# The last K tile of an fp32 operand's low part at another place within 256 bytes

## The reference

```python
u = x @ w_in                                  # 2048 -> 6144 columns
mix = concatenate([a_out, b_out]) @ w_out     # 2048 -> 2048
x = layer_norm(ALPHA * x + mix)
h = square(relu(x @ mlp_w1)) @ mlp_w2         # 2048 -> 8192 -> 2048
x = layer_norm(ALPHA * x + h)
```

## Time and profile before

| | |
|---|---|
| median of 3 runs | 2264.65 us |
| the profiled execution, its own time | 2263.86 us |
| its span, first to last instruction | 2262.1 us |
| PE busy | 2230.1 us, 99% |
| DVE busy | 1334.3 us, 59% |
| ACT busy | 1043.3 us, 46% |
| mean share of the DMA engines, first queue | 55.4% |
| granted TensorE clock, mean | 0.996 |

### The profile page before, as it was taken

The page is one execution under the profiler, slowest core; times in us unless marked ns, Lnnn a source line. Parts: engine busy times, 40 slices in busy tenths (PEclk is TensorE's granted clock), DMA queues, the critical chain, the costliest instruction groups (busy, mean ns, idle before and its releaser), DMA issues.

```text
span 2262.1 us, 36589 instructions
## 1 busy us (share of the span) xinstructions
PE 2230.1 (99%) x14395; PEld 2022.1 (89%) x14395; DVE 1334.3 (59%) x1472; ACT 1043.3 (46%) x1133; POOL 36.5 (2%) x68
## 2 busy tenths in 40 slices
PE   8999999999999999999999999999999999999998
PEld 8998888798898899899889999888989988988986
DVE  4999977854544545444565455568555454545455
ACT  4555565454444344354434444444544444544542
POOL 2000000000000001000000000000000000000000
PEclk9999999999999999999999999999999999999999
DMA  6555535565656566555536655564656566555553
GB/s 234 177 161 153 183 131 166 185 218 195 203 188 211 199 197 197 201 179 195 187 125 201 186 169 169 166 215 153 215 191 196 196 216 203 185 187 197 178 195 112
DMA packets 213081, 419.17 MB, mean 185 GB/s; under 512 B 12793, under 2 KB 13361, under 8 KB 211904
## 3 DMA queue, kind: packets, MB, share of 16 engines
q1 hardware_dynamic: 210832, 406.37, 55.4%
q0 software_dynamic: 1808, 10.04, 1.3%
q10 hardware_dynamic: 288, 0.52, 0.1%
HBM read 414.79 MB, written 2.10 MB: 184 GB/s over the span
## 4 chain that ended last, share of the span: by engine, by line
PE 92%; DVE 5%; issue 1%; DMA 1%; ACT 1%; SPq 0%; DVEq 0%; ACTq 0%
PE gemm L1343 15%; PE gemm L1345 15%; PE gemm L1344 15%; PE gemm L1367 14%; PE gemm L1370 14%; PE gemm L1369 14%; DVE lnp L1087 2%; DVE w_lo L806 1%; PE pair L1506 1%; DMA raw<-in_ev_w_in 1%; PE pair L1467 0%; DMA raw<-in_mlp_w 0%; PE pair L1565 0%; PE pair L1637 0%; PE pair L1610 0%
## 5 line engine op out<-in xcount | busy, mean ns | idle before, releaser
L1216 DVE TENSOR_TENSOR w_lo<-raw,w_hi 128x1024 fp32r<-128x1024 f32 x488 | 594.5, 1225 | 560.4 <-ACT w_hi L719 545.3
L1367 PE MATMUL gemm<-x_hi,w_hi 128*128 128x256 f32 x2944 | 824.9, 280 | 4.6 <-DVE w_lo L806 2.4
L719 ACT ACTIVATE w_hi<-raw 128x1024 fp32r<-128x1024 f32 x492 | 518.3, 1060 | 672.2 <-PE gemm L1345 375.4
L1370 PE MATMUL gemm<-x_hi,w_lo 128*128 128x256 f32 x2944 | 822.5, 279 | 0.1
L1369 PE MATMUL gemm<-x_lo,w_hi 128*128 128x256 f32 x2944 | 822.4, 279 | 0.0
L1367 PEld LDWEIGHTS gemm<-x_hi,w_hi 128*128 128x128 f32 x2944 | 554.2, 188 | 7.6 <-issue 2.9
L1370 PEld LDWEIGHTS gemm<-x_hi,w_lo 128*128 128x128 f32 x2944 | 560.8, 190 | 0.3 <-issue 0.3
L1369 PEld LDWEIGHTS gemm<-x_lo,w_hi 128*128 128x128 f32 x2944 | 554.7, 188 | 0.5
L1343 PE MATMUL gemm<-w_hi,c_hi 128*128 128x512 f32 x1280 | 501.0, 391 | 1.3 <-DVE w_lo L806 1.0
L1344 PE MATMUL gemm<-w_lo,c_hi 128*128 128x512 f32 x1280 | 499.1, 390 | 0.0
L1345 PE MATMUL gemm<-w_hi,c_lo 128*128 128x512 f32 x1280 | 499.1, 390 | 0.0
(11 more groups left out here) (191 smaller groups left out, 940.2 us busy)
## 6 DMA issues: line engine op xcount, KB each, us to landing
raw<-in_mlp_w SPq DMA_DIRECT2D x512, 512.0 KB, 4.4
raw<-in_ev_w_in SPq DMA_DIRECT2D x96, 512.0 KB, 4.3
raw<-in_od_w_in SPq DMA_DIRECT2D x96, 512.0 KB, 3.9
raw<-in_ev_w_out SPq DMA_DIRECT2D x32, 512.0 KB, 4.2
raw<-in_od_w_out SPq DMA_DIRECT2D x32, 512.0 KB, 4.0
lnp<-in_ln_mix_g POOLq DMA_DIRECT2D x2, 1024.0 KB, 7.1
lnp<-in_ln_mix_b POOLq DMA_DIRECT2D x2, 1024.0 KB, 8.5
lnp<-in_ln_mlp_g POOLq DMA_DIRECT2D x2, 1024.0 KB, 4.8
```

The lines of the kernel that those rows point to most:

```text
L719: act.activation(hi_of_chunk(s), raw[:, s % RING], ACT.Copy).then_inc(hi_ready, 1)
L1216: dve.tensor_tensor(lo_of_chunk(s), raw[:, s % RING], hi_of_chunk(s).bitcast(F32), ALU.subtract).then_inc(lo_ready, 1)
L1367: pe.matmul(acc[:, m, :], high, hi[:, k + c, :], start=begin and m % 2 == 0, stop=False, skip_group_check=True)
L1370: ins = pe.matmul(acc[:, m, :], low, hi[:, k + c, :], start=False, stop=end and m % 2 == 1, skip_group_check=True)
```

## The change

c_lo gets 48 more columns (192 bytes a partition), and its last K tile, k = 15, starts that much higher: at byte 64 within 256 instead of 128. The other 15 K tiles stay where they were. before_X, another 64 bytes that nothing uses, follows it, so that X, the layer-norm parameters, the scratch, w_hi2, w_lo2 and all behind lie 256 bytes higher and keep their places within 256. As the last K tile no longer joins the one before, every DVE instruction that wrote k = 12 to 15 becomes two: three K tiles, and the last. All writers of c_lo go through `c_lo_from`; the matmuls take their K tile from functions instead of slices, which changes no instruction on PE but for the place of c_lo[15].

```diff
+C_GAP = 48
+def c_lo_tiles(c_lo, k0, n):
+    assert k0 == KT - 1 or k0 + n < KT
+    start = k0 * S + (C_GAP if k0 == KT - 1 else 0)
+    return c_lo[:, start:start + n * S].rearrange("p (k t) -> p k t", k=n)
+def c_lo_runs(k0, n):
+    return [(k0, n - 1), (KT - 1, 1)] if k0 + n == KT else [(k0, n)]
...
-        c_lo = sb("c_lo", [P, KT, S], F32R)
+        c_lo = sb("c_lo", [P, KT * S + C_GAP], F32R)
+        before_X = sb("before_X", [P, 16], F32)
...
+            def c_lo_from(src, k0, n):
+                for k, n_ in c_lo_runs(k0, n):
+                    ins = dve.tensor_tensor(c_lo_tiles(c_lo, k, n_), src[:, k - k0:k - k0 + n_, :],
+                                            c_hi[:, k:k + n_, :].bitcast(F32), ALU.subtract)
+                return ins
...
             def group_lo(k0, value):
-                lo_of(0, c_hi[:, k0:k0 + 4, :], c_lo[:, k0:k0 + 4, :], cat_hi, value, cat_ready)
+                dve.wait_ge(cat_hi, value)
+                c_lo_from(quad[0], k0, 4).then_inc(cat_ready, 1)
...
-                    dve.tensor_tensor(c_lo[:, 4 * (i - 1):4 * i, :], quad[0] if by_rows and i == 1 else h_turned[(i - 1) % 2],
-                                      c_hi[:, 4 * (i - 1):4 * i, :].bitcast(F32), ALU.subtract
-                                      ).then_inc(h_ready, 1)
+                    c_lo_from(quad[0] if by_rows and i == 1 else h_turned[(i - 1) % 2], 4 * (i - 1), 4).then_inc(h_ready, 1)
...
-            C_ = (c_hi, c_lo)
+            C_ = (lambda k: c_hi[:, k, :], lambda k: c_lo_tiles(c_lo, k, 1)[:, 0, :])
```

More of the change, by code:

```diff
@@ L1151, in _ @@
                     dve.wait_ge(cat_hi, 2)
-                    dve.tensor_tensor(c_lo[:, 0:8, :], csq, c_hi[:, 0:8, :].bitcast(F32), ALU.subtract
-                                      ).then_inc(cat_ready, 1)
+                    c_lo_from(csq, 0, 8).then_inc(cat_ready, 1)
                 if s == LEVEL_SLOT[1] + 25:
@@ L1298, in _ @@
                     upto(s0 + 10)
-                    lo_of(0, c_hi[:, 4 * (g - 1):4 * g, :], c_lo[:, 4 * (g - 1):4 * g, :], cat_hi, 3 + g, cat_ready)
+                    group_lo(4 * (g - 1), 3 + g)
                 if g == 0:
@@ L1331, in _ @@
             upto(o + 110)
-            lo_of(0, c_hi[:, 12:16, :], c_lo[:, 12:16, :], cat_hi, 7, cat_ready)
+            group_lo(12, 7)
             mix_norm(1)
@@ L1342, in products @@
                 high, low = hi_of_chunk(s)[:, c, :], lo_of_chunk(s)[:, c, :]
-                pe.matmul(acc[:, r, :], hi[:, k + c, rows], high, start=begin, stop=False)
-                pe.matmul(acc[:, r, :], hi[:, k + c, rows], low, start=False, stop=False)
-                return pe.matmul(acc[:, r, :], lo[:, k + c, rows], high, start=False, stop=end)
+                pe.matmul(acc[:, r, :], hi(k + c)[:, rows], high, start=begin, stop=False)
+                pe.matmul(acc[:, r, :], hi(k + c)[:, rows], low, start=False, stop=False)
+                return pe.matmul(acc[:, r, :], lo(k + c)[:, rows], high, start=False, stop=end)
             def chunk_rows(acc, act_, r, k, s, first, last, halfway=None):
@@ L1366, in turned_chunk @@
                         high, low = hi_of_chunk(s)[:, c, cols], lo_of_chunk(s)[:, c, cols]
-                        pe.matmul(acc[:, m, :], high, hi[:, k + c, :], start=begin and m % 2 == 0, stop=False,
+                        pe.matmul(acc[:, m, :], high, hi(k + c), start=begin and m % 2 == 0, stop=False,
                                   skip_group_check=True)
-                        pe.matmul(acc[:, m, :], high, lo[:, k + c, :], start=False, stop=False, skip_group_check=True)
-                        ins = pe.matmul(acc[:, m, :], low, hi[:, k + c, :], start=False, stop=end and m % 2 == 1,
+                        pe.matmul(acc[:, m, :], high, lo(k + c), start=False, stop=False, skip_group_check=True)
+                        ins = pe.matmul(acc[:, m, :], low, hi(k + c), start=False, stop=end and m % 2 == 1,
                                         skip_group_check=True)
@@ L1490, in tile_behind_norm @@
                                        halfway=(lambda n=n: row_piece(which, n)) if n else None)
-            X_ = (x_hi, x_lo)
-            C_ = (c_hi, c_lo)
+            X_ = (lambda k: x_hi[:, k, :], lambda k: x_lo[:, k, :])
+            C_ = (lambda k: c_hi[:, k, :], lambda k: c_lo_tiles(c_lo, k, 1)[:, 0, :])
             at = [0, 0]
```

## The result

| | before | after |
|---|---|---|
| median, range, runs | 2259.61 us (2258.15 to 2269.71), 7 | 2247.95 us (2246.46 to 2252.04), 7 |
| ratio of the two | | 0.9946 [0.9933, 0.9960] |
| the profiled execution | 2263.86 us | 2247.95 us |
| its span | 2262.1 us | 2246.2 us |

What follows compares the result with a forecast made beforehand. PE, busy 99% of the span, bounds the kernel, so only matmul pitch can gain. 2263.86 - 20.3 + 1.6 + 0.2 = 2245.4 us, plus 0.8 toward the runs' median gives 2246 us (chance 0.58); 8-in-10 range 2240 to 2268 us.

Steps and rivals of the forecast that it cites:

- The mechanism: At W1 entries behind W2, c_lo[15] loaded at byte 64 turns six long-pace blocks short: 20.5 us, 20.3 after entry costs.
- its signs: In later blocks' W1: matmul duration 276, weight load 188, pitch 113.4 ns, stage 87.1 us; last W2 matmul over 0.23 us.
- the number of blocks: All six W1 blocks behind a first block, three in each layer, were counted as turning short, 20.5 us in all.
- a rival, at half of all blocks: W1 entries: offset also depends on stops, so about half the blocks turn short; gain 10.1 us, 2256 us, chance 0.12.
- What the displaced load costs: In W2 and w_out tiles, c_lo[15] is loaded 80 times at about 20 ns each: 1.6 us in all.
- At the pace from x for good: Slower rival: W2 and w_out streams stay at 229.0 ns, W1 stays long; costs 8.5 us, 2273 us, chance 0.07.
- The split: DVE's two writes instead of one take 157 ns more, hidden in the MLP, 0.16 us exposed in layer 0's mixer.
- The 256 bytes: Everything behind c_lo lies 256 bytes higher; a step of 256 was claimed to have no effect: 0.
- The entry's own cost: At W1's entry behind W2, a longer last matmul and five pitches of 116 to 117 ns cost about 25 ns.
- An ordinary entry keeps the offset: PE's weight loads and stream hold a fixed offset; an ordinary entry keeps it, one load at another place shifts it.
- Theories A and C: Experiment with x at 128: last stationary load must lie 64 bytes below earlier loads (A, 2256 to 2259 us) or at x's place (C, 2263).

## Why the prediction came out right, step by step

- **The mechanism held**, with its signs: duration 276, weight load 188, 0.23 us before the entry, 87.06 us a stage. With x at 64 and c at 128, entries that are not the loop's turn and have c_lo's last load one step of 64 bytes off: 24 of 24 short (three profiles with the loop, four each; two with it written out, six each). With it in step, two steps off, or displaced three matmuls earlier: 22 of 22 long. The Trainium skill's rule of two independent ports ("TensorE: Matmul & The Clock Gate", section "Part 2: What happens when you issue a matmul"), by which the place of a stationary operand would not matter, doesn't agree with these streams: 0.9946 with one K tile moved by 192 bytes, 1.0004 with it moved back.
- **The term that was mis-sized is the number of blocks.** The sum took six blocks at 3.4 us. Full for each it was, 20.3 us with the loop written out, but the change got 16.4: one block and part of another were lost to the loop's stops. The earlier trace rows showed such stops, and the prediction filed them under a rival, at half of all blocks, instead of asking which entries have a loop's turn ahead of them. It is one entry in three, in both layers; two entries of 3.4 us at even odds would have put the forecast 3.4 us higher. Nor are these two long before the change in every execution: of the four profiles with the loop and no last load one step off, layer 0's was short in two, layer 1's, behind its second stop, in three. What the change is sure of is four entries, 13.6 us.
- **What the displaced load costs** was right: 20 ns forecast, 20 to 21 measured. A W2 tile with two of them takes 21.80 us instead of 21.76. The table's 1.11 us, 17 ns for each of 64, is less because before's W2 also holds a stop of 0.3 us. "At the pace from x for good" did not happen: four matmuls later the stream is back at 226 to 227 ns.
- **The split** was too dear: 0.06 us instead of 0.16, because two writes in a row overlap on DVE; in layer 0's mixer PE did not wait for it at all in this profile. Too small to tell in the time.
- **The 256 bytes** cost nothing (1.0004 with the place taken back).
- **The entry's own cost**, 25 ns, was right: 236 instead of 226 ns, and 17 ns over the next five pitches.
- **The two errors that hid each other.** The forecast of 2246 us stood on a median of 2264.65. Measured side by side, before has 2259.61 to 2263.09 in the four sets of several runs, so the gain is 12 to 15 us, not 18.6, and the 4 to 7 us of gain that are missing met a before that was 2 to 5 us faster than its first three runs. The time is right to 0.1%; the gain was put too high by a quarter to six tenths.
- **"An ordinary entry keeps the offset"** stays a reading. What is shown is that the entry depends on the place of the last load, that a stop decides anew, and that the loop's turn can do so with 20 ns or no visible stop; how loads and stream get out of each other's way, no run shows. Theories A and C, made from it for x's place, fell.

## What to carry to other kernels

Where PE is busy all the time, compare the pitch of the same instruction in several stages; two paces in equal streams are a place to look, and the entry into each is read from the timeline. Move one operand at a time by 64 bytes within 256 and measure all four places, since their paces follow no rule that could be guessed here. Count the stops that a hardware loop puts into such a stream before you count all its turns as gained.

## What was not expected of the hardware

- A turned fp32r stream of 256 columns ran at 113.3, 117.8, 118.7 or 120.0 ns with the same instructions and a mean granted clock of 0.996 to 0.997 in every profiled execution, by the place of the streamed operand and by how it was entered; by rows, 512 columns, at 226.8 to 233.3.
- With x at 64 and c at 128, a single weight load one step off, at the end of W2, sets the pace of the next 768 matmuls; moved by two steps, or three matmuls earlier, it does not.
- A stop of 70 ns at a loop's turn cost 3.5 us behind it, 50 times itself.
